# A first weight unit and a norm's gain row with homes of their own, loaded one stage earlier, and a ring of four raw slots

## The reference

```
def reference(...):
    x = first_block(x, c, ada_w, ..., final_norm_g)
    return second_block(x, w_in_2, conv_a_w_2, ..., ln2_g_2, ln2_b_2)
```

```
def rms_norm(x, g):
    xf = x.astype(jnp.float32)
    y = xf * lax.rsqrt(jnp.mean(xf * xf, axis=-1, keepdims=True) + NORM_EPS)
    return (y * g.astype(jnp.float32)).astype(x.dtype)
```

## Time and profile before

| | us |
|---|---|
| median of 3 runs | 1788.2 |
| lowest, highest | 1785.66, 1788.42 |
| the profiled execution's own time | 1779.32 |
| its span | 1777.6 |
| PE busy | 1585.3 (89%) |
| DVE busy | 1222.9 (69%) |
| ACT busy | 817.9 (46%) |
| POOL busy | 45.4 (3%) |
| end of the last down product, of x, start of the mixer's first products | 912.97, 916.05, 931.68 |

### The profile page before, as it was taken

How to read it: one execution, slowest core, us unless ns; L and a number is a source line. 1 busy time by engine, 2 the same in 40 slices (tenths; PEclk the granted TensorE clock), 3 DMA queues, 4 the chain that set the end, 5 groups by cost and what they waited for, 6 DMA issues and landing times. The chain is left out here.

```text
span 1777.6 us, 25493 instructions
## 1 busy us (share of the span) xinstructions
PE 1585.3 (89%) x10701; PEld 1436.9 (81%) x10701; DVE 1222.9 (69%) x1352; ACT 817.9 (46%) x952; POOL 45.4 (3%) x60
## 2 busy tenths in 40 slices
PE   2899998899989999899969999687689979999995
PEld 2789988799888988899959898686678777888884
DVE  4877586888756648756545785633566868899895
ACT  1345543343344554444333465223453346777774
POOL 0100000000020000000000000000000000000000
PEclk9999999999989999999989999897898989999998
DMA  8974435999855324666536563111232537999993
GB/s 305 325 238 146 162 121 168 341 327 320 283 153 157 119 96 142 202 204 217 173 87 190 157 190 119 49 47 48 72 95 72 176 134 250 379 358 372 364 356 121
DMA packets 226056, 348.05 MB, mean 196 GB/s; under 512 B 14612, under 2 KB 156672, under 8 KB 225808
## 3 DMA queue, kind: packets, MB, share of 16 engines
q1 hardware_dynamic: 225936, 346.36, 58.0%
HBM read 345.29 MB, written 1.97 MB: 195 GB/s over the span
## 5 line engine op out<-in xcount | busy, mean ns | idle before, releaser
L459 PE MATMUL bank<-layer_split,hT_pair 128*128 128x256 f32 (+2 forms) x4032 | 513.5, 287 | 30.2 <-DVE hT_pair L1035 20.9
L459 PEld LDWEIGHTS bank<-layer_split,hT_pair 128*128 128x128 f32 x4032 | 487.1, 191 | 44.3 <-issue 28.8
L184 DVE TENSOR_TENSOR layer_split<-layer_raw,layer_split 128x2048 fp32r<-128x2048 f32 x122 | 279.6, 2292 | 105.2 <-ACT layer_split L172 103.6
L172 ACT ACTIVATE layer_split<-layer_raw 128x2048 fp32r<-128x2048 f32 x122 | 233.6, 1915 | 193.7 <-PE bank L459 78.8
L184 DVE TENSOR_TENSOR expert_split<-expert_raw,expert_split 128x2048 fp32r<-128x2048 f32 x96 | 219.0, 2288 | 26.4 <-ACT expert_split L172 26.0
L172 ACT ACTIVATE expert_split<-expert_raw 128x2048 fp32r<-128x2048 f32 x96 | 183.4, 1917 | 55.8 <-PE bank L2476 31.4
L459 PE MATMUL bank<-split_w,hT_pair 128*128 128x256 f32 (+1 forms) x1248 | 169.1, 296 | 9.2 <-ACT mixer_arena L2783 3.2
L459 PEld LDWEIGHTS bank<-split_w,hT_pair 128*128 128x128 f32 x1248 | 158.1, 195 | 19.8 <-issue 11.3
L184 DVE TENSOR_TENSOR split_w<-raw_w,split_w 128x2048 fp32r<-128x2048 f32 x52 | 119.2, 2292 | 61.2 <-ACT split_w L172 60.5
L1898 PE MATMUL bank<-layer_split,ffnh_aT 128*128 128x512 f32 x528 | 127.0, 396 | 2.8 <-DVE ffnh_aT L1970 2.8
L459 PE MATMUL bank<-hT_pair,split_w 128*128 128x256 f32 x960 | 119.6, 285 | 5.2 <-DVE hT_pair L315 4.6
(11 more groups left out here) (466 smaller groups left out, 1891.7 us busy)
## 6 DMA issues: line engine op xcount, KB each, us to landing
layer_raw<-in_ada_w SPq DMA_DIRECT2D x48, 1024.0 KB, 6.5
layer_raw<-in_ffn_w_gate_up SPq DMA_DIRECT2D x44, 1024.0 KB, 5.7
raw_w<-in_w_in SPq DMA_DIRECT2D x40, 1024.0 KB, 5.4
layer_raw<-in_w_in SPq DMA_DIRECT2D x38, 1024.0 KB, 6.5
expert_raw<-in_w_gate SPq DMA_DIRECT2D x32, 1024.0 KB, 7.2
expert_raw<-in_w_up SPq DMA_DIRECT2D x32, 1024.0 KB, 7.4
expert_raw<-in_w_down SPq DMA_DIRECT2D x32, 1024.0 KB, 7.0
layer_raw<-in_ffn_w_down SPq DMA_DIRECT2D x22, 1024.0 KB, 5.2
```

The lines of the kernel that those rows point to most:

```text
L172: self.nc.scalar.activation(self.pair[:, j % self.pairs, 0, 0:self.size[n]], self.raw[:, n % self.depth, 0:self.size[n]], ACT.Copy).then_i ...
L184: self.nc.vector.tensor_tensor(self.pair[:, j % self.pairs, 1, 0:self.size[n]], self.raw[:, n % self.depth, 0:self.size[n]], self.pair[:, ...
L459: ins = nc.tensor.matmul(out, lhs, rhs, start=first and c == chunks[0] and tp + wp == 0, stop=last and c == chunks[-1] and tp == 1)
```

## The change

Two buffers are made for the whole program: `last_gain` (128 x 1024) and `first_unit` (128 x 2048), with a semaphore each. At the end of SP's program for the second layer's feed-forward (the one with no norm to follow in its block) the gain row and the mixer's unit 0 are loaded into them. The mixer's ring takes `first_unit` as its slot 0 ahead of the three slots of `raw_w`, so it has four, with unit 0 counted as issued; units 4, 8 and so on are later loaded into the same buffer. The norm reads the gain row from its new home. `Merge` and `FeedForward` share one step semaphore instead of having one each. Every buffer that is made after the two lies 12,288 bytes per partition higher than before.

```diff
@@ class Ring
-    def __init__(self, nc, name, raw, pair, units, scaled=(), scale=None, acc=None, pieces=None):
-        self.nc, self.units, self.raw, self.pair = nc, units, raw, pair
+    def __init__(self, nc, name, raw, pair, units, scaled=(), scale=None, acc=None, pieces=None, early=None):
+        self.nc, self.units, self.pair = nc, units, pair
+        self.raw = [raw[:, i, :] for i in range(raw.shape[1])]
+        if early is not None:
+            self.raw.insert(0, early[0])
...
-        self.depth, self.pairs = raw.shape[1], pair.shape[1]
-        self.landed = [new_sem(nc, f"{name}_landed{s}") for s in range(self.depth)]
+        self.depth, self.pairs = len(self.raw), pair.shape[1]
+        self.landed = [new_sem(nc, f"{name}_landed{s}") if s or early is None else early[1] for s in range(self.depth)]
...
-        self.issued = self.split_hi = self.split_lo = 0
+        self.issued = 0 if early is None else 1
+        self.split_hi = self.split_lo = 0
...
@@ program
+        last_gain, first_unit = sb("final_gain", [P, D]), sb("first_unit_raw", [P, UNIT])
+        gain_loaded, first_unit_in = new_sem(nc, "final_gain_loaded"), new_sem(nc, "second_landed0")
...
@@ LayerBuffers, Merge, FeedForward
+                self.step = Count(nc, "layers_dve_step")
...
-                self.left, self.out_left, self.step = (Count(nc, f"merge_{n}") for n in ("branch_left", "out_left", "step"))
+                self.left, self.out_left = (Count(nc, f"merge_{n}") for n in ("branch_left", "out_left"))
+                self.step = buf.step
...
-                self.step, self.added = Count(nc, "ffnh_step"), Count(nc, "ffnh_added")
+                self.step, self.added = buf.step, Count(nc, "ffnh_added")
@@ FeedForward.sync
                 self.ring.feed(sp, self.ring.ahead(self.dn(self.blocks - 1), 2))
+                if self.norm_next is None:
+                    sp.dma_start(last_gain[:, :], A["final_norm_g"].rearrange("(o n) -> o n", o=1).broadcast_to([P, D])) \
+                        .then_inc(gain_loaded, 16)
+                    sp.dma_start(first_unit[:, :].rearrange("p (k n) -> p k n", k=KD), cols2("w_in_2", 0, 256)) \
+                        .then_inc(first_unit_in, 16)
@@ second_part
-                ring = Ring(nc, "second", sb("raw_w", [P, 3, UNIT], st), sb("split_w", [P, 2, 2, UNIT], st, FR), units)
+                ring = Ring(nc, "second", sb("raw_w", [P, 3, UNIT], st), sb("split_w", [P, 2, 2, UNIT], st, FR), units,
+                            early=(first_unit[:, :], first_unit_in))
@@ mixer
-                raw, gain = arena(13 * D, P), work_[:, 1, :]
...
                 def load_first(sp):
-                    sp.dma_start(gain[:, :], A["final_norm_g"].rearrange("(o n) -> o n", o=1).broadcast_to([P, D])) \
-                        .then_inc(gain_loaded, 16)
                     ring.feed(sp, -1)
...
-                norm = Norm("final", s2, ring, U_A[0], row_gain=gain[:, :], late_gain=(gain_loaded, 16), junk=work_[:, 0, :])
+                norm = Norm("final", s2, ring, U_A[0], row_gain=last_gain[:, :], late_gain=(gain_loaded, 16), junk=work_[:, 0, :])
```

More of the change, by code:

```diff
@@ L157, in feed @@
             for at, k, width, c0, c1, src in self.units[n]:
-                dst = self.raw[:, n % self.depth, at:at + k * width].rearrange("p (k n) -> p k n", k=k)[:, :, c0:c1]
+                dst = self.raw[n % self.depth][:, at:at + k * width].rearrange("p (k n) -> p k n", k=k)[:, :, c0:c1]
                 sp.dma_start(dst, src).then_inc(self.landed[n % self.depth], 16)
@@ L172, in hi @@
             self.nc.scalar.activation(self.pair[:, j % self.pairs, 0, 0:self.size[n]],
-                                      self.raw[:, n % self.depth, 0:self.size[n]], ACT.Copy).then_inc(self.hi_done, 1)
+                                      self.raw[n % self.depth][:, 0:self.size[n]], ACT.Copy).then_inc(self.hi_done, 1)
     def lo(self, dve, through):
@@ L184, in lo @@
             self.nc.vector.tensor_tensor(self.pair[:, j % self.pairs, 1, 0:self.size[n]],
-                                         self.raw[:, n % self.depth, 0:self.size[n]],
+                                         self.raw[n % self.depth][:, 0:self.size[n]],
                                          self.pair[:, j % self.pairs, 0, 0:self.size[n]].bitcast(FP),
@@ L192, in accumulate @@
         acc = self.acc[g]
-        first, second = (self.raw[:, n % self.depth, i * D:(i + 1) * D] for i in range(2))
+        first, second = (self.raw[n % self.depth][:, i * D:(i + 1) * D] for i in range(2))
         dve.wait_ge(self.landed[n % self.depth], self.value[n])
@@ L2816, in load_lru @@
                     sp.wait_ge(tables_loaded, 16)
-                raw, gain = arena(13 * D, P), work_[:, 1, :]
-                gain_loaded, raw_loaded, rest_loaded, tables_loaded = (new_sem(nc, n) for n in
-                    ("final_gain_loaded", "raw_2_loaded", "small_2_loaded", "tables_loaded"))
+                raw = arena(13 * D, P)
+                raw_loaded, rest_loaded, tables_loaded = (new_sem(nc, n) for n in
+                    ("raw_2_loaded", "small_2_loaded", "tables_loaded"))
                 def load_first(sp):
-                    sp.dma_start(gain[:, :], A["final_norm_g"].rearrange("(o n) -> o n", o=1).broadcast_to([P, D])) \
-                        .then_inc(gain_loaded, 16)
                     ring.feed(sp, -1)
```

## The result

| us | before | changed |
|---|---|---|
| median of 5 runs | 1785.66 | 1776.13 |
| lowest, highest | 1784.84, 1788.42 | 1774.98, 1779.01 |
| the profiled execution's own time | 1779.32 | 1777.70 |
| its span | 1777.6 | 1775.8 |

The two profiled executions differ by only 1.8 us in span. Both numbers need an explanation, and it is not the same one.

A forecast was written before the change was run, and what follows sets the result against it. Unit 0's load was taken to bound the seam, the gain row next, with PE busy 89% of the span. 4.3 us saved less 0.2 for the clock gave 4.1: 1788.2 to 1784.1 us, range 1781.4 to 1787.8.

The forecast's parts named there:

- the seam: Stretch between the layers and the mixer where PE stands; without its two load waits 4.3 us are saved.
- Unit 0's load: Start of the mixer: ACT's split waits 5.5 us for it; it bounds, hiding the norm's 6.3 us gain-row wait.
- The early loads: Behind the layers' last ring loads on SP: both in place by about 885, 36 us cover, no cost.
- POOL's root: Tile 1's root in the norm, beside DVE's L381: L259 takes 0.99 us instead of 0.19; unhindered, 5.1 us saved, chance 0.15.
- The low half: DVE's part of unit 0's split: starts some 5.4 us behind the block's start instead of 9.8.
- the first products: PE's first gated products in the mixer: 9.3 us behind the block's start instead of 13.6.
- The memset: POOL's L2805 beside tile 1's L381: costs nothing, at most 0.95 us; chance 0.15 that it or the clock takes a part.
- The fourth slot: Mixer's ring: each load issued at the same moment but carrying the next unit; cost and gain nothing.
- the moved addresses: Buffers 12,288 bytes higher: no effect forecast; rival of slower matmuls or loads, 10.7 us per ns, chance 0.05.
- The shared semaphore: Step semaphore shared by Merge and FeedForward: leaves every wait where it was, nothing.
- the clock's term: TensorE's clock at half when ungated products begin: 0.2 us lost, bounds nothing to 1.0 us.
- the runs' error: Uncertainty of a timed median, about 1.4 us, half the spread of three runs; used for chances and range.

The follow-up runs named there:

- unit 0 alone: Changed kernel with the gain row's DMA back at the start of the mixer's block, only unit 0 loaded early; ratio 0.9974 against the kernel before.
- With three slots: Changed kernel with two slots in raw_w, three in all, a spare buffer replacing the third; median 1776.6 us, ratio 0.9963 against the kernel before.
- the spacers: Kernel before plus two unused buffers, so every later buffer lies 12,288 bytes higher; median 1785.7 us, ratio 1.0010 against the kernel before.
- the later sets: Three sets of runs after the first, on three different chips, each kernel timed beside the kernel before; changed kernel unedited: ratios 0.9969, 0.9971, 0.9957.
- third set: Changed kernel without edits, timed again beside the kernel before; 1779.0 against 1784.3 us, ratio 0.9971.
- second set: Changed kernel without edits, timed again beside the kernel before; ratio 0.9969, 3.6 us faster by the medians.
- first set: Original comparison, five runs each of changed kernel and kernel before, no chip on record; medians 1776.13 against 1785.66 us, ratio 0.9944.

## Why the prediction was right, and where it was wrong

**Right: the seam.** Its steps came out one by one. Unit 0's load was the bound and the gain row's next (rows above, unit 0 alone: 6.46 us). The early loads land long before they are used, the gain row 6.1 us behind its issue. POOL's root is stretched beside L381's successor and the second multiplication waits for it, as rows 6 had it: 0.99 us in both places. The low half came at 5.35 us (forecast 5.4), the first products at 9.18 (forecast 9.3). The memset, whose full length beside DVE no row had shown, cost nothing: both took their usual 0.95 and 1.28 us side by side. By what the Trainium skill says (SBUF — State Buffer, "Who interferes with whom"), that a two-input DVE instruction contends with GpSimd's reads and not with its writes, the trace agrees on both counts. The fourth slot and the moved addresses gave nothing that could be measured. The shared semaphore was not tried by itself.

**Wrong, small: the clock's term.** I took 0.2 us off the gain, for a clock that might be at half when the ungated products begin. In the four profiles of the changed kernel that did not happen: from the low half to the first copy it is 11.74 or 11.75 us each time (925.67 to 937.42 in the first). The windows of the first, from the gated products on (PE, PEld, DVE, ACT, POOL busy, PEclk, DMA share, GB/s):

```profile
928.00:930.00 2.00, 0.50 (x2) 0.54 (x3) 1.97 (x5) 2.00 (x3) 0.00 (x0) 0.50 1.09 347
930.00:932.00 2.00, 2.00 (x11) 2.00 (x10) 1.93 (x5) 0.40 (x1) 0.00 (x0) 0.50 1.22 219
932.00:934.00 2.00, 1.97 (x12) 1.73 (x11) 1.97 (x5) 0.00 (x0) 0.00 (x0) 0.73 0.32 25
934.00:936.00 2.00, 2.00 (x19) 2.00 (x18) 1.73 (x1) 0.39 (x1) 0.00 (x0) 1.00 0.57 121
```

The clock did not rise during the transposes, as it had in the kernel before; it stayed at half (1.2 GHz) and rose once, at about 933.1, 3.6 us behind the first products and 0.5 us before the ungated ones. In the other three it stayed at half as long and rose 3.3 to 3.8 us behind the first products. So the term was nothing here. With three slots, the seam otherwise the same, it did rise during the transposes, fell again and was back at full 4.2 us behind the first products, which cost 0.02 us: the place of the transposes alone does not fix it.

It is the kernel before that pays. From the low half to the first copy its profiled execution, the one I had, took 11.74; the two others and the spacers took 12.5 to 12.7. In all four the clock rose within 0.5 us behind the end of the transposes, fell again before the first products, and rose a second time: 3.0 us behind the first products in the profile that I had, 5.8 to 6.1 us behind them in the three others. In one of those it is at 0.50 (1.2 GHz) for ungated products too:

```profile
937.00:939.00 2.00, 2.00 (x10) 1.96 (x10) 2.00 (x2) 0.00 (x0) 0.00 (x0) 0.50 0.98 314
```

So the seam is worth 4.4 us against the profile that I read and up to 5.5 against others; of the 1.1 us between, 0.8 are the clock's, and 0.3 come from a later landing of unit 0 in that execution. The mean of the four profiles without the early loads is 22.2, 5.1 us more than 17.1. Why the second rise came late in three of the four is open. PE stands 4.3 to 4.6 us between transposes and products there (4.3 in the earlier trace rows) and 1.7 in the changed kernel, but no run varied that pause alone.

**Wrong, and what put the result outside the range: the runs' error.** The step reads "A median here is uncertain by about 1.4 us (half the spread of the three)". It was too small by half and left a part out. The 107 runs of the kernel before in the later sets have a standard deviation of 4.1 us; medians of three of them scatter by 2.9, and the changed kernel's median of five adds 2.4 of its own, 3.7 together. The miss, 1784.1 - 1776.1 = 8.0 us, is 2.1 times that. Of the 8.0, 2.5 are the starting point, since the first median fell from 1788.2 with three runs to 1785.7 with five, and 5.4 are the difference between the kernels, 9.5 instead of 4.1. Runs of one program lie up to 17 us apart, and the profile itself was the warning: it was 8.9 us under the median, more than three times the spread of the three runs, and I took that for an offset instead of a second draw from a wide distribution. A part of the spread is seen in two profiles of the changed kernel, third set and second set, in the stretch of GLA (the recurrence in chunks of 16 tokens) from the masked scores (L3629) to the third head's first state (L3643). The windows of PE alone (busy, count, PEclk, DMA share, GB/s), first 1774.8 us of span:

```profile
1319.40:1340.60 21.20, 20.34 (x179) 1.00 0.25 87
1436.80:1458.40 21.60, 12.66 (x96) 0.75 0.62 221
```

and 1786.1 us:

```profile
1322.30:1348.30 26.00, 25.14 (x179) 0.80 0.25 82
1445.30:1470.30 25.00, 16.05 (x97) 0.69 0.60 210
```

The same 179 matmuls take 4.8 us more while the granted clock is 0.80 in the mean; single groups show it, the 24 products of one job at full and at half:

```profile
1329.93 3.01 PE L465 MATMUL bank<-split_w,hT_pair 128*128 128x256 f32 x24
```

```profile
1333.54 5.49 PE L465 MATMUL bank<-split_w,hT_pair 128*128 128x256 f32 x24
```

The second line of each pair is the stretch of the layer norm and the routing, 3.4 us longer in the second profile. Together 8 of the 11 us between the two executions. In 12 profiles GLA is long (26.0 to 27.5 us) in five: one of the five without unit 0's early load (the spacers), four of the seven with it. The kernel before is short in all three of its profiles, the changed kernel in two of four. So in these profiles the change does not make the fall rarer. Whether it makes it more frequent, 12 profiles are too few to tell. The side is taken earlier than the stretch: in all seven short executions the clock is at half for some 3 us between 5 and 1 us before it, and then at full throughout; in all five long ones that happens 6 us earlier, between 11 and 7 us before it, and the clock falls twice more inside it. What decides between the two courses no run here shows.

The 12 profiles also tell what lies outside the seam: the span less the way from the block's start to the first copy. It is 1756.1, 1759.4 and 1757.0 us in the kernel before and 1758.7, 1769.0, 1757.7 and 1764.0 in the changed kernel, 1769.0 and 1764.0 with the long GLA stretch. No gain stands there; the profiles show one at the seam only.

Pooled over my three sets, the kernel before has a mean of 1784.1 us in 107 runs (standard error 0.4), the changed kernel 1779.7 in 31 (0.7): 4.4 us, with an interval of 2.9 to 6.0. Set by set it is 3.4, 4.5 and 5.9. That holds the forecast of 4.1 and the seam's 4.4 to 5.5. The first set's 9.5 us are 4 to 5 us more than the seam gives.

**What stays open.** That the first set's remaining 4 to 5 us come from which executions fell on the good side is the likeliest reading, since the same program's executions lie 10 us apart with the seam unchanged. It is argued, not shown: the profile of each kernel in that set is a single one, both with the short GLA stretch, and the kernel before was never profiled with the long one. Five and five runs drawn at random from the later sets have medians 9.5 us or more apart about once in 20 draws, so chance alone does it, but seldom. Consecutive runs may also share a side, which would make an interval from five runs too narrow; the five runs of either kernel in the first set have a standard deviation of 1.7 us, the later ones about 4. An effect beyond the seam of 1 or 2 us isn't excluded either. A kernel that keeps the clock at full through GLA, which would tell, was not tried.

No version here beats the changed kernel by more than the runs can tell; the one with three slots does as well with 8 KB per partition less.

## What to carry to other kernels

A load at the head of a stage is better issued in the stage before, if its target can have a home there; look also at what stands in front of the load that is waited for, since half a MB ahead of it cost 2.3 us here though its own wait was hidden. Price such an edit by the distance between two events in the trace, which repeated to 0.01 us, and not by whole times, which moved by 17; and take a profile that lies far from the timed median as a sign of how wide the times are, and widen the range by it. When a wait goes, ask which instructions now run side by side that had not before.

## What had not been expected of the hardware

- The granted clock fell within the GLA stage in some executions and not in others, with the same instructions in the same order ahead of it: 26.0 against 21.2 us. The two courses differ already between 11 and 7 us before the stretch, where only the long executions are at half clock. The Trainium skill (TensorE: Matmul & The Clock Gate, "Part 1: The HAM clock gate") has it that the gate runs free of the kernel, which would make this a matter of chance. The runs agree in so far as the changed kernel showed both lengths, two profiles each; the kernel before showed the short one in all three.
- The same 16 transposes were followed within 0.5 us by the clock at full in the kernel before (three profiles) and with the spacers, and left it at half (1.2 GHz) in the four profiles of the changed kernel, where they start 3.5 us behind the block's start instead of 5.4 to 5.8. With three slots they start at 3.5 us too, and the clock rose all the same, so this place alone does not decide it.
- A load of 1 MB landed 5.48 us behind the block's start when first in the queue and 7.78 behind a row of 0.5 MB; 0.4 of the 2.3 us between is SP's issue. In the three further profiles with the row in front it was 7.8 to 8.1.
